# Attention: the strips of heads 0 and 1 computed between matmuls of the last four Q units

## What is computed

```
q = _rmsnorm((h @ b_w_q).reshape(B, S, N_HEADS, HEAD_DIM), q_norm_g)
z = einsum("bhtd,bhsd->bhts", qb, kb) * scale
log_beta = log_sigmoid(z)
log_keep = where(causal, log_sigmoid(-z), 0.0)
between = cumsum(log_keep, axis=3, reverse=True) - log_keep
weights = where(causal, exp(log_beta + between), 0.0)
outs.append(einsum("bhts,bhsd->bhtd", weights, vb))
```

## Time and profile before

| | us |
|---|---|
| median of 3 runs | 2614.03 |
| lowest and highest | 2613.42, 2614.82 |
| the profiled execution, its own time | 2611.83 |
| its span | 2609.8 |
| TensorE busy in the span | 2528.0 |
| VectorE, ScalarE, GpSimd busy | 1582.7, 985.7, 148.7 |

### The profile page before, as it was taken

The page is one execution under the profiler, slowest core; times in us unless marked ns, Lnnn a source line. Parts: engine busy times, 40 slices in busy tenths (PEclk is TensorE's granted clock), DMA queues, the critical chain, the costliest instruction groups (busy, mean ns, idle before and its releaser), DMA issues.

```text
span 2609.8 us, 33660 instructions
## 1 busy us (share of the span) xinstructions
PE 2528.0 (97%) x12220; PEld 2062.6 (79%) x12220; DVE 1582.7 (61%) x1907; ACT 985.7 (38%) x1423; POOL 148.7 (6%) x151
## 2 busy tenths in 40 slices
PE   6999999999999999999999997999999999999999
PEld 4878778888888878888898886666788888888887
DVE  6877766568877666666623634777258665544442
ACT  5543343235454431111311333777335544321110
POOL 0000000000000000000000002666000000000000
PEclk9999999999999999999999997999999999999999
DMA  6344564313344475554142353654322323632311
GB/s 254 104 151 153 177 222 171 115 49 129 125 165 155 164 273 199 187 203 139 45 156 83 105 177 89 132 125 107 137 89 97 129 100 113 259 118 81 113 49 70
DMA packets 122980, 359.60 MB, mean 138 GB/s; under 512 B 12032, under 2 KB 28416, under 8 KB 118912
## 3 DMA queue, kind: packets, MB, share of 16 engines
q1 hardware_dynamic: 122880, 358.23, 40.9%
HBM read 270.10 MB, written 88.08 MB: 137 GB/s over the span
## 4 chain that ended last, share of the span: by engine, by line
PE 79%; DVE 8%; DMA 6%; ACT 4%; issue 3%; SPq 1%; DVEq 0%; ACTq 0%; POOL 0%; POOLq 0%
PE PS L2033 22%; PE PS L2035 22%; PE PS L2034 22%; DMA RAW<-in_wt 2%; DVE KEEP L1953 2%; PE PS L2513 2%; PE PS L2500 2%; DMA MODRAW<-in_modw 1%; PE PS L2481 1%; PE PS L2137 1%; ACT PS L1267 1%; PE PS L2139 1%; PE PS L2138 1%; PE PS L2437 1%; PE PS L2482 1%
## 5 line engine op out<-in xcount | busy, mean ns | idle before, releaser
L2033 PE MATMUL PS<-HID_HI,W_HI 128*128 128x512 f32 x1024 | 400.1, 391 | 5.5 <-DVE HID_LO L1602 4.9
L2034 PE MATMUL PS<-HID_LO,W_HI 128*128 128x512 f32 x1024 | 398.6, 389 | 0.0
L2035 PE MATMUL PS<-HID_HI,W_LO 128*128 128x512 f32 x1024 | 398.5, 389 | 0.0
L374 ACT ACTIVATE W_HI<-RAW 128x1024 fp32r<-128x1024 f32 x114 | 119.5, 1059 | 615.7 <-PE PS L2035 509.9
L1448 DVE SCALAR_TENSOR_TENSOR X<-PS,MODV,X 128x1024 f32<-128x1024 f32 x124 | 159.1, 1283 | 300.1 <-PE PS L2035 291.7
L2033 PE MATMUL PS<-H_HI,W_HI 128*128 128x512 f32 x700 | 277.7, 397 | 3.3 <-DVE H_LO L1392 2.2
L2035 PE MATMUL PS<-H_HI,W_LO 128*128 128x512 f32 x700 | 273.5, 391 | 0.0
L2034 PE MATMUL PS<-H_LO,W_HI 128*128 128x512 f32 x700 | 273.3, 390 | 0.0
L2033 PEld LDWEIGHTS PS<-HID_HI,W_HI 128*128 128x128 f32 x1024 | 192.2, 188 | 49.5 <-DVE HID_LO L1602 7.9
L2035 PEld LDWEIGHTS PS<-HID_HI,W_LO 128*128 128x128 f32 x1024 | 192.2, 188 | 40.2
L2034 PEld LDWEIGHTS PS<-HID_LO,W_HI 128*128 128x128 f32 x1024 | 192.2, 188 | 39.7 <-issue 0.2
(11 more groups left out here) (223 smaller groups left out, 4928.8 us busy)
## 6 DMA issues: line engine op xcount, KB each, us to landing
RAW<-in_wt SPq DMA_DIRECT2D x208, 512.0 KB, 4.2
MODRAW<-in_modw SPq DMA_DIRECT2D x96, 512.0 KB, 3.4
HRAW<-hid_scratch SPq DMA_DIRECT2D x14, 2048.0 KB, 9.1
hid_scratch<-TN SPq DMA_DIRECT2D x90, 256.0 KB, 2.8
hid_scratch<-SCR SPq DMA_DIRECT2D x84, 256.0 KB, 3.8
x_scratch<-X SPq DMA_DIRECT2D x3, 4096.0 KB, 13.9
X<-x_scratch SPq DMA_DIRECT2D x6, 2048.0 KB, 9.3
QK<-qk_scratch SPq DMA_DIRECT2D x16, 768.0 KB, 6.3
```

Of the source, the lines that this page charges most:

```text
L374: act.activation(ring_view(W_HI, n), raw_view(n), ACT.Copy).then_inc(sem["w_hi"], 1)
L2033: pe.matmul(dst, w_hi, m_hi, start=first, stop=False)
L2034: pe.matmul(dst, w_hi, m_lo, start=False, stop=False)
L2035: return pe.matmul(dst, w_lo, m_hi, start=False, stop=last)
```

## The change

The eight strips of each of heads 0 and 1 leave the attention. They are numbered 0 to 15 in the order EARLY (head 0: strips of 1024, 512, 896, 384, 768, 256, 640, 128 columns; then head 1 alike). Their scores, 48 matmuls, are set into the units 12 to 15 (`late_q_unit`, which takes the place of `wide_unit`). A unit has eight points, one behind every six matmuls; EARLY_AT gives the point of each strip, counted from the start of unit 12: 5, 7, 9, 10, 12, 14, 16, 17, 19, 21, 23, 24, 26, 28, 30, 31. The head sums stand at the fourth point, where they stood. The scores go into banks 4 and 5 (strips wider than 512) or bank 6, in turn, and a strip n waits on PE for the scan of strip n - 2. Sigmoid, scan and difference have their places in the periods 12 to 15 of ACT and DVE and in POOL's queue; the products lie in KEEP_E, the differences in A_E.

The attention starts with pair 1, with `back` pair 0, whose turns read A_E. The first two pieces of head 2 and the last unit's head sums (now in bank 6) are made before PE waits for the last Q unit's banks. The last unit's root and reciprocal move from head 0 to head 2. SP stores unit 10 ahead of two weight loads, and loads the QK rows of head 2 ahead of the last store.

The table of places, and SP's queue:

```diff
+EARLY = [(h, b) for h in range(2) for b in (0, 4, 1, 5, 2, 6, 3, 7)]
+EARLY_AT = [5, 7, 9, 10, 12, 14, 16, 17, 19, 21, 23, 24, 26, 28, 30, 31]
...
             for c in range(2 * KT + 1):
+                if c == KT + 3:
+                    kq_store(c - 1)
...
-                if c > KT:
+                if c > KT and c != KT + 3:
                     kq_store(c - 1)
+                if c == 2 * KT - 1:
+                    sp.wait_ge(sem["kq_out1"], 32 * 6)
+                    sp.wait_ge(sem["z_full"], STEPS)
+                    load_qk(Count(1), 0)
...
-            next_qk(Count(0), Count(1), 0)
             next_qk(Count(1), Count(1), 1)
```

POOL, then ACT; DVE has `early_stick` and `kq_inverse` in the same places of its period:

```diff
+            for n, (h, b) in enumerate(EARLY):
+                w = S - P * b
+                pool.wait_ge(sem["scanned"], n + 1)
+                pool.tensor_tensor(A_E[h][b][:], KEEP_E[n % 4][:, 0:w], KEEP_E[n % 4][:, 1:w + 1], ALU.subtract
+                                   ).then_inc(sem["a_ok"], 1)
...
+                for n in early_in(c, 0, 3):
+                    early_sig(n)
                 if 0 < c < 2 * KT:
                     kq_root(c - 1)
+                for n in early_in(c, 3, KT):
+                    early_sig(n)
+
+            def early_sig(n):
+                h, b = EARLY[n]
+                z = early_scores(n)
+                act.wait_ge(sem["z_full"], EARLY_PIECES[n])
+                act.activation(z, z, ACT.Sigmoid, scale=RQ[:, 2 * b + h:2 * b + h + 1]).then_inc(sem["keep_ok"], 1)
...
-                    if h.c == 0 and s == 3:
+                    if h.c == 2 and s == 3:
                         kq_root(2 * KT - 1)
                         act.wait_ge(sem["kq_rec"], 2 * KT)
```

DVE's scan, and PE:

```diff
+            def early_stick(n):
...
+                dve.wait_ge(sem["keep_ok"], n + 1)
+                if n >= 4:
+                    dve.wait_ge(sem["a_ok"], n - 3)
+                dve.tensor_tensor_scan(KEEP_E[n % 4][:, 1:1 + w], early_scores(n), MASK[:, 0:w], 1.0, ALU.mult, ALU.max
+                                       ).then_inc(sem["scanned"], 1)
...
+            def early(n):
+                h, b = EARLY[n]
+                if n % 8 == 0:
+                    pe.wait_ge(sem[f"qk_in{h}"], 48)
+                if n > 1:
+                    pe.wait_ge(sem["scanned"], n - 1)
...
+                for part in range(2 if b < 4 else 1):
+                    c = b * P + part * HALF
+                    w = min(S - c, HALF)
+                    dst = PS[:, 4 + part if b < 4 else 6, 0:w]
+                    pe.matmul(dst, q, QK[:, h, 0, c:c + w], start=True, stop=False)
+                    pe.matmul(dst, q, QK[:, h, 1, c:c + w], start=False, stop=True).then_inc(sem["z_full"], 1)
+
+            def late_q_unit(c):
...
+                        if k % 2:
+                            point = 4 * half + k // 2
+                            if point == 3:
+                                head_sums(c - 1)
+                            for m in early_in(c, point, point + 1):
+                                early(m)
...
-            for c in range(12, 16):
-                wide_unit(Count(T_K + c), Count(U_K + c), H_HI, H_LO, lambda: head_sums(c - 1))
+                late_q_unit(c)
...
+            pe.wait_ge(sem["acc_free"], freed(U_O - 2))
+            scores(Count(2), 0, 0, True)
+            scores(Count(2), 0, 1, True)
+            head_sums(2 * KT - 1)
             pe.wait_ge(sem["acc_free"], freed(U_O - 1))
-            pe.wait_ge(sem["ident_ok"], 2)
-            pair_phases(Count(0), None, None, None, True)
-            pair_phases(Count(1), Count(0), 0, None, False)
+            pair_phases(Count(1), Count(0), 0, None, True)
```

More of the change, by code:

```diff
@@ L141, with early_in @@
 assert len(PIECES) == STEPS
+EARLY = [(h, b) for h in range(2) for b in (0, 4, 1, 5, 2, 6, 3, 7)]
+EARLY_AT = [5, 7, 9, 10, 12, 14, 16, 17, 19, 21, 23, 24, 26, 28, 30, 31]
+EARLY_PIECES = [sum(2 if b < 4 else 1 for h, b in EARLY[:n + 1]) for n in range(len(EARLY))]
+def early_in(c, first, stop):
+    return [n for n, at in enumerate(EARLY_AT) if c * KT + first <= at + 12 * KT < c * KT + stop]
 class Count:
@@ L309, in build @@
                 for b in range(4)]
+        KEEP_E = [at(f"KEEP_E{b}", [P, w + 8], F32, off) for b, (w, off) in enumerate(
+            ((1024, RX + 24 * KB), (512, RB + 56 * KB), (896, RX + 24 * KB + 4128), (384, RB + 56 * KB + 2080)))]
+        A_E = [[at(f"A_E{h}_{b}", [P, S - P * b], F32, RB + off) for b, off in enumerate(offs)] for h, offs in enumerate((
+            [4 * STRIP[b] for b in range(KT)],
+            [18 * KB, 36 * KB, 36 * KB + 3584, 44 * KB, 22 * KB, 46 * KB + 512, 36 * KB + 6656, 36 * KB + 7680]))]
         VH = at("VH", [P, 2, NCHUNK, P], F32, RH + 51 * KB)
@@ L863, in head @@
                                        ALU.subtract).then_inc(sem["a_ok"], 1)
-            for b in range(4):
+            for b in range(2, 4):
                 head(Count(b), b, None)
@@ L2465, in _ @@
             quad(Count(T_Q), Count(U_Q), H_HI, H_LO, 48, halfway(8))
+            def early(n):
+                h, b = EARLY[n]
+                if n % 8 == 0:
+                    pe.wait_ge(sem[f"qk_in{h}"], 48)
+                if n > 1:
+                    pe.wait_ge(sem["scanned"], n - 1)
+                if n == 0:
+                    pe.wait_ge(sem["kq_norm"], KT)
+                q = QK[:, h, 2, b * P:(b + 1) * P]
+                for part in range(2 if b < 4 else 1):
[5 more added lines that the diff above has]
+            def late_q_unit(c):
+                n, u = T_K + c, U_K + c
+                s, slot = n % RING, u % 2
+                pe.wait_ge(sem["w_lo"], tiles_cut(Count(n)).v)
+                pe.wait_ge(sem["acc_free"], freed(u - 2))
+                for half in range(2):
+                    sl = half_of(half)
+                    for k in range(KT):
+                        mm = three(PS[:, 2 * slot + half, :], W_HI[:, k, s * P:(s + 1) * P],
+                                   W_LO[:, k, s * P:(s + 1) * P], H_HI[:, k, sl], H_LO[:, k, sl], k == 0, k == KT - 1)
+                        if half and k == KT - 1:
+                            mm.then_inc(sem["acc_full"], 1)
+                        if k % 2:
[4 more added lines that the diff above has]
+                                early(m)
             for c in range(12, 16):
-                wide_unit(Count(T_K + c), Count(U_K + c), H_HI, H_LO, lambda: head_sums(c - 1))
+                late_q_unit(c)
             def scores(h, par, s, first):
@@ L2487, in turn @@
                 h = pair * 2 + x
-                if q == 0:
+                if first and n == 0:
+                    pe.wait_ge(sem["a_ok"], len(EARLY))
+                    pe.wait_ge(sem["kq_sqrt"], 2 * KT - 1)
+                elif q == 0:
                     pe.wait_ge(sem["a_ok"], (h * KT + 4).v)
-                    if first:
-                        pe.wait_ge(sem["kq_norm"], KT)
-                        pe.wait_ge(sem["kq_sqrt"], 2 * KT)
                 if q == 8:
@@ L2499, in turn @@
                     c = STRIP[t] + (j - t) * P
[L2500 removed]
+                    block = A_E[x][t][:, (j - t) * P:(j - t + 1) * P] if first else A[2 * b + x][:, c:c + P]
+                    mm = pe.transpose(PS[:, TURNED[n % 3], m * P:(m + 1) * P], block, IDENT[:])
                 mm.then_inc(sem["at_full"], 1)
@@ L2507, in weigh @@
                     pe.wait_ge(sem[f"v_in{b}"], ((pair // 2) * 16 + 16).v)
+                    if pair.i is None and pair.c == 0:
+                        pe.wait_ge(sem["kq_sqrt"], 2 * KT)
                 if j == KT - 1 and (g == 1 or pair.i is not None or pair.c > 0):
@@ L2520, in phase @@
                         turn(back, n, b, before is None)
-                    if h.c < HEADS:
+                    if h.c < HEADS and not (first and par == 0 and s < 2):
                         scores(h, par, s, first)
-                    if h.c == 0 and s == 0:
-                        head_sums(2 * KT - 1)
                     if n % 4 == 1 and back is not None:
```

33 lines of the change are left out of this document (24 added, 9 removed).

## The result

The changed kernel takes **2587.1 us** (median of 4 runs, 2584.26 to 2591.76) against 2613.73 for the kernel before on the same chip (4 runs, 2609.2 to 2614.82). The ratio is 0.9903, 95% interval 0.9884 to 0.9922, a gain of 26.6 us. The prediction said 2593.0 and a range from 2588.5.

The account below looks back on a forecast made before the run. PE's time was taken to bound the kernel, with the chain of heads 0 and 1 exposed. Terms 9.0 + 0 + 4.4 + 2.5 = 15.9 us replace 36.9, gaining 21.0: 2593.0 us, range 2588.5 to 2602.

Parts of the forecast that it names:

- The exposed piece: From last Q matmul to first transposition: 36.9 us, from which the chain of heads 0 and 1 goes.
- Term a: In Q units 12 to 15: the 48 inserted score matmuls add 9.0 us to PE's path, between 8.3 and 10.9.
- Waits for scans: In the Q units: inserted scores make PE wait 0 us for scans, upper bound 7, tightest margin 0.6.
- The first rival: In the Q units: PE does wait for scans behind late squares or table loads, 4 to 7 us, 2599; chance 0.10.
- Table loads: On ACT: nine table changes instead of three, each 1.28 us, with no drain counted.
- The second rival: At ACT's table switches: each costs more than its load, taken as 2.56 us, giving 2599.5; chance 0.04.
- QK rows of heads 0 and 1: Unit 12: with the store moved ahead, loads land by 1549, wanted about 1552; 0 us of waiting, bound 2.
- Term b: Hand-over from last Q matmul to pair 0's first turned strips: 4.4 us, between 4.0 and 5.
- Term c: Last root and reciprocal in head 2 delay its third scan by 3.7 us; 2.5 stays, between 1.0 and 5.
- The third rival: In head 2, behind the hand-over: PE idles and its clock drops to 1.2 GHz, 4 us, 2597; chance 0.08.
- The fourth and the fifth rival: Pair 0's weighings: V or QK rows late, 5 us, chance 0.04; Q units: clock lost, 2632, chance 0.03.
- How the numbers follow: Step from sum to whole time: predicted 2593, range 2588.5 to 2602, gains of 25.5 to 12; chance 0.68.

Follow-up runs that it names:

- store_back: The changed kernel with unit 10's store put back behind the two weight loads on SP: 2587.99 us, ratio 0.9912.
- before_pad: The kernel before with 48 two-column matmuls added behind the last projection at PE's end: 2621.06 us, ratio 1.0042.
- act_no_wait: The changed kernel with ACT's wait for the last root's reciprocal moved from head 2 to head 3: 2583.51 us, ratio 0.9897.
- after_c: The changed kernel, unaltered, profiled once more for the time of its first V matmul: 2585.22 us.
- before_b: The kernel before, unaltered, timed and profiled again on another chip: 2610.45 us, ratio 0.9999.
- root_first: The changed kernel with the last root and reciprocal ahead of head 2, the reciprocal's wait in head 3: 2584.34 us, ratio 0.9913.
- loads_first: The changed kernel with last root and reciprocal ahead of head 2, and head 2's QK rows and pair 0's V loaded before stores: 2586.04 us, ratio 0.9911.
- half_scores: The changed kernel without the second matmul of each score piece of heads 0 and 1 (24 of 48): 2585.56 us, ratio 0.9909.

## Why the prediction was right where it was, and where it failed

- **The exposed piece** (36.9 us): confirmed, 36.9 and 36.4 in two profiles each. It became 4.6.
- **Term a** (9.0, ends 8.3 and 10.9): 8.6 in each profile. The four times of the second row of the table hold 0.7 more on average, and that isn't from the insertion: two of the four changed profiles lose 1.2 to 1.5 us within the V stage, before any score, where the clock falls (below).
- **Waits for scans** (0, bound 7): none. PE is busy 59.51 of 59.51 us. The first rival is out.
- **Table loads** (nine of 1.28): nine, each 1.283 us. In the rows above the load at 1557.20 is over before its root's head sums exist, and the root follows them at once: that load costs nothing at all. The drain of the Trainium skill ("ScalarE: Activation LUTs", What ACT_TABLE_LOAD costs) shows in no row, as in the earlier trace rows: 1611.66 plus 1.28 is 1612.94, and the sigmoid starts at 1612.96. PE is full in the Q units, so no strip was stalled by a load either. The second rival is out.
- **QK rows of heads 0 and 1** (in time): in time, and store_back shows that without the moved store they would have been 0.9 late. The estimate behind this step ("that would be just late") held.
- **Term b** (4.4, ends 4.0 and 5): 4.5 to 4.7. The QK rows of pair 1 are 1.6 us late, "beside head sums" as the text has it, and V 1.0 or less.
- **Term c** (2.5, ends 1.0 and 5): 1.8 on average, from 220.0 to 221.8. Its step by step path holds closely: the third scan at 12.59 and 11.70 us where 12.4 was worked out (before, it stood at 8.6 or 8.7 us in two profiles and at 9.9 in the two whose clock was down longer); ACT waits 2.29 us for a product of 1.61 us that ends with POOL's difference. That is the shape that the text predicted from the earlier trace rows.
- **The third rival** (clock falls behind the hand-over): it occurs, in one of four profiles, 0.57 in the first 4 us of the pairs (the windows above). Its price was put at 4 us; there the first scan of head 3 comes at 21.6 us instead of 20.7, so 0.9.
- **The fourth and the fifth rival** (V or QK rows land late, the clock is lost in the Q units): out, with waits of 1.0 us or less for V and a granted clock of 1.00 in the Q units.
- **The sum** (15.9 in place of 36.9, gain 21.0): 15.7 in place of 36.6, gain 20.9, over four profiles each. That it meets so closely is in part luck: the second stage is 0.3 over term a (0.7 of it the clock in the V stage), b 0.2 over its term, c 0.7 under.

**The step that failed** is the one from the sum to the time, "How the numbers follow". It set the new time against the median of three runs that lay within 1.4 us of each other (2613.42 to 2614.82), and built the range from the ends of the terms alone. It also took the stages ahead of the change to stay as they were, without a reason given. Of 68 distinct times of the kernel before, on all chips used, the lowest is 2604.2, the highest 2616.6, the mean 2609.6, with a standard deviation of 2.7; the three that I had belong to the upper part. The 13 runs of the changed kernel have a mean of 2585.9, the same deviation of 2.6, and reach from 2583.2 to 2591.8. Put together: 2609.6 less 20.9 is 2588.7; the first V matmul comes on average 2.6 us earlier in the changed profiles (1275.2 against 1277.8), which leads to 2586.1. So of the 5.9 us by which 2593.0 missed 2587.1, 4.4 were in the base, the terms were 0.1 off the other way, and the remaining 1.6 are the first stages together with the spread of four runs. A base with its own spread of some 5 us would have put the low end near 2584.

Why those three were high is open. Of the other 65 times only five reach 2613.42, so three in a row are hardly chance. The four runs of the changed kernel in the first comparison are high as well, 2587.6 on average against 2584.0 and 2586.1 in the two later ones. A difference from chip to chip or from hour to hour would do this; no run here parts the two from chance.

**What stays open** is why the first stages are 2.6 us faster on average. They lie before anything that the change touches, and their values overlap (1273.6 to 1278.6, and 1275.8 to 1279.9; the five edited versions of the changed kernel 1271.7 to 1276.9, before_pad 1274.0). before_pad's times speak against the length of PE's program as the cause. Eight profiles don't exclude chance, but the means of all times stand 23.7 us apart, 2.8 more than the touched stages give, with a standard error of 0.8 (2.6 over the root of 13 with 2.7 over the root of 68; differences between chips are not in it). Within each of the three comparisons the means stand 25.3, 24.8 and 23.5 us apart. I don't know what it is.

## What to carry to other kernels

A chain that is exposed because no neighbour exists yet at a stage's start can be set into the stage before it; its price was then the matmuls' issue there, since each piece's wait was shorter than the work set between the pieces. Work it out stage by stage from marker to marker, and compare such stages, not whole spans: here the touched stages together, from the first V matmul to the end, agreed to 1 us between profiles of a kernel while the spans moved by 4 to 5. And take the base from many runs, with its own spread. Where PE has gaps, taking away a wait beside them may not be worth its length: in act_no_wait 2.7 us became 0.6, with the clock down behind the gap that was left. Look at the granted clock of the next few us before counting the saving.

## What the runs showed of the hardware that I had not expected

- **A V stage that takes 102.4 or 103.8 us in the same kernel.** From the first V matmul to the last one on two high halves pass 102.5 us in all four profiles of before, and 102.4, 104.0, 102.5 and 103.7 in the changed ones. PE alone, in 8 us from the first V matmul and in 8 us from the first matmul behind the stage's gap of 3.6 us (length, busy, count, clock, share, GB/s), of after_c and then of before_b:

```profile
1273.60:1281.60 8.00, 6.22 (x35) 0.79 0.19 69
1353.10:1361.10 8.00, 8.00 (x54) 0.79 0.53 145
```

```profile
1279.90:1287.90 8.00, 6.01 (x45) 1.00 0.19 69
1358.17:1366.17 8.00, 8.00 (x54) 0.79 0.52 150
```

  Behind the gap of 3.6 us the clock falls to 1.2 GHz (half of 2.4) in both alike: 54 matmuls in 8 us, where a full 8 us has 69. The difference lies at the start. There PE waits 1.0 and 0.7 us for DVE's low halves in every profile, and behind these two waits the clock falls in some (35 matmuls in after_c) and not in others (45 in before_b). It fell in five of the nine profiles of the changed kernel and its edits and in none of the five of before and before_pad; whether that is chance is open.
- **Dropped waits that gain nothing that the times can show.** Four edits (act_no_wait, root_first, loads_first, half_scores) removed 1 to 4 us each of waiting or work in the Q units, at the hand-over or in head 2, and the medians, 2583.5 to 2586.0, are not to be told from the changed kernel's 2584.0 to 2587.1.
- **Two-column matmuls at a program's end.** 48 of them, each in two passes, took 15.1 us from the first start to the last, 0.31 each, and lengthened the run by 11.3. The granted clock fell beside them, from 1.00 in their first 4 us (38 passes) to 0.50 in their third (21 passes). At the full clock the eight head sums of two columns take 1.70 us, 0.21 each. Being short did not make them free.
